# Seven products of blocks instead of eight in the MLP's second product, over three quarters of its weight rows

## The reference

```python
h = rmsnorm_2(x, g_norm2[l]) * (1.0 + sc2) + sh2
x = x + gt2 * (jnp.square(jax.nn.relu(h @ w1[l])) @ w2[l])
```

## Time and profile before

| | |
|---|---|
| median of 3 runs | 994.14 us (993.88 to 995.94) |
| the profiled execution: its own time | 994.67 us |
| its span, first to last instruction | 992.8 us |
| PE busy | 974.2 us (98%) |
| DVE busy | 656.1 us (66%) |
| ACT busy | 483.6 us (49%) |
| granted TensorE clock, mean | 0.999 |

### The profile page before, as it was taken

The page is one execution under the profiler, slowest core; times in us unless marked ns, Lnnn a source line. Parts: engine busy times, 40 slices in busy tenths (PEclk is TensorE's granted clock), DMA queues, the critical chain, the costliest instruction groups (busy, mean ns, idle before and its releaser), DMA issues.

```text
span 992.8 us, 13022 instructions
## 1 busy us (share of the span) xinstructions
PE 974.2 (98%) x4784; PEld 813.3 (82%) x4784; DVE 656.1 (66%) x1203; ACT 483.6 (49%) x963; POOL 69.9 (7%) x158
## 2 busy tenths in 40 slices
PE   9999999999999999999899999999999999999998
PEld 7878999888888888777788878788888888888886
DVE  6487888869788758367678886875455544445453
ACT  6458777753223445589787554343224214322420
POOL 4001001012112011000000001100000000000000
PEclk9999999999999999999999999999999999999999
DMA  8205131248778415342442226147222232322221
GB/s 299 77 23 183 65 104 58 86 181 329 281 289 318 175 79 154 101 145 80 138 148 65 70 101 254 43 168 151 85 85 85 90 121 85 127 85 85 85 75 53
DMA packets 34080, 129.81 MB, mean 131 GB/s; under 512 B 8905, under 2 KB 8905, under 8 KB 24418
## 3 DMA queue, kind: packets, MB, share of 16 engines
q1 hardware_dynamic: 23538, 98.27, 29.3%
q0 software_dynamic: 7408, 26.75, 7.9%
q10 hardware_dynamic: 3072, 3.98, 1.2%
HBM read 119.45 MB, written 5.27 MB: 126 GB/s over the span
## 4 chain that ended last, share of the span: by engine, by line
PE 82%; DVE 9%; ACT 4%; issue 2%; DMA 2%; POOL 0%; SPq 0%; DVEq 0%; ACTq 0%; POOLq 0%
PE psum L1849 24%; PE psum L1851 24%; PE psum L1850 24%; PE psum L2016 2%; PE psum L1995 2%; PE psum L2045 1%; PE psum L2048 1%; DVE wl L1088 1%; DVE two L1627 1%; PE psum L1883 1%; DVE hl L1128 1%; DMA value_rows<-rows 1%; ACT wh L589 1%; DVE two L1492 1%; DMA raw<-in_wall 1%
## 5 line engine op out<-in xcount | busy, mean ns | idle before, releaser
L1849 PE MATMUL psum<-hh,wh 128*128 128x512 f32 (+1 forms) x720 | 274.0, 381 | 0.7 <-DVE hl L1128 0.6
L1851 PE MATMUL psum<-hh,wl 128*128 128x512 f32 (+1 forms) x720 | 267.4, 371 | 0.0
L1850 PE MATMUL psum<-hl,wh 128*128 128x512 f32 (+1 forms) x720 | 267.2, 371 | 0.0
L589 ACT ACTIVATE wh<-raw 128x512 fp32r<-128x512 f32 x292 | 169.3, 620 | 137.3 <-PE psum L1851 121.7
L1088 DVE TENSOR_TENSOR wl<-raw,wh 128x512 fp32r<-128x512 f32 x292 | 192.1, 683 | 16.7 <-ACT wh L589 16.4
L1849 PEld LDWEIGHTS psum<-hh,wh 128*128 128x128 f32 x720 | 135.3, 188 | 24.3 <-DVE hl L1128 1.6
L1851 PEld LDWEIGHTS psum<-hh,wl 128*128 128x128 f32 x720 | 135.2, 188 | 23.8
L1850 PEld LDWEIGHTS psum<-hl,wh 128*128 128x128 f32 x720 | 135.5, 188 | 21.1 <-issue 1.0
L1849 PE MATMUL psum<-wh,ah 128*128 128x512 f32 x320 | 125.6, 392 | 0.0
L1851 PE MATMUL psum<-wh,al 128*128 128x512 f32 x320 | 124.6, 389 | 0.0
L1850 PE MATMUL psum<-wl,ah 128*128 128x512 f32 x320 | 124.6, 389 | 0.0
(11 more groups left out here) (282 smaller groups left out, 1464.9 us busy)
## 6 DMA issues: line engine op xcount, KB each, us to landing
raw<-in_wall SPq DMA_DIRECT2D x75, 1024.0 KB, 5.0
wa<-in_wada POOLq DMA_DIRECT2D x20, 512.0 KB, 6.3
gt<-in_wada POOLq DMA_DIRECT2D x20, 512.0 KB, 6.4
wb<-in_wada POOLq DMA_DIRECT2D x8, 512.0 KB, 7.7
xt<-in_xcols SPq DMA_DIRECT2D x8, 264.0 KB, 7.8
cb<-c_rows SPq DMA_DIRECT2D x8, 264.0 KB, 3.3
x<-in_x SPq DMA_DIRECT2D x4, 512.0 KB, 10.2
x_kept<-x SPq DMA_DIRECT2D x4, 512.0 KB, 2.8
```

The source lines that it names most:

```text
L589: e.activation(home(w)[0][:, 512 * c:512 * c + 512], raw_of(w, c), ACT.Copy).then_inc(a["wh"], 1)
L1849: e.matmul(out_, lh, rh, start=start, stop=False, skip_group_check=True)
L1850: e.matmul(out_, lh, rl, start=False, stop=False, skip_group_check=True)
L1851: return e.matmul(out_, ll, rh, start=False, stop=stop, skip_group_check=True)
```

## The change

In quarters 0, 1 and 2 the second product is done by Strassen's scheme. With A the squares of a quarter (512 tokens by 1024 hidden) and B its 1024x1024 rows of `w2`, A and B are cut into 2x2 blocks (A11 is 256 tokens by 512 hidden, B11 is 512x512, one unit). PE makes seven products, in this order of numbers: 1, 2, 7, 6, 5, 3, 4.

- Each product is 2 token tiles x 4 k tiles x 3 = 24 matmuls of 128x512.
- Products 1, 2, 3 use the units B11, B21, B22 as loaded. Products 7, 6, 5, 4 use sums and differences of units, each made from the one before in the raw buffers by DVE, in two instructions of 128x1024 (`weight_sum`).
- The activations get their sums too (`halves`): one difference of 256 columns for hidden tiles 0 to 3, three dependent ones for tiles 4 to 7, of which a tile of 768 columns is split again (`s_hi`, `s_lo`).
- Products 3 and 4 stay in banks 4 to 7 over the three quarters. Products 1, 2, 7, 6, 5 are added up over the quarters in SBUF: in quarter 0 by an ACT copy (`first_sum`), in quarters 1 and 2 by a DVE add (`gather`), two instructions for each product.
- In quarter 3, whose product is done as before, DVE combines the seven sums into the four blocks (`blocks`, 14 instructions), multiplies by the gate and adds to `x2` (`add_block`, 16 instructions), and does so again for quarter 3's own product (`add_last`). The eight gated steps at the end of quarters 0 to 2 are gone.
- There is a fourth raw buffer, `raw3`, which lies over `mis`; its first load waits for the last of the table sums. Raw buffers are held until the last sum that needs them has been split (`place`, `freed`). The order of loading in `w2` is B11, B22, B12, B21.
- The slots in which the MLP's lower parts stand are moved by one or so, and some semaphores are merged under one name (`n1` and `n3` into `nsq`, `hh1` and `hh2` into `hh`, `hl1` and `hl2` into `hl`, `tp1` and `tp2` into `tp`).

The diff, cut to its core:

```diff
+PRODUCTS = (1, 2, 7, 6, 5, 3, 4)
+P_BANK = {1: (2, 3), 2: (0, 1), 7: (2, 3), 6: (0, 1), 5: (2, 3), 3: (4, 5), 4: (6, 7)}
+GATHERED = (1, 2, 7, 6, 5)
...
+        for w_ in range(W_MLP + 1, NW):
+            lowers[w_] = {1: (0,), 3: (1,), 5: (2,), 6: (3,)}
...
+                    if place[n] == 3 and nth[n] == 1:
+                        e.wait_ge(v["tile"], 48)
...
+            def hidden_upper(n, part=0):
+                q, m = divmod(n, 8)
+                if q < 3 and (m < 4 or part):
+                    e.wait_ge(v["s"], 16 * q + (m + 1 if m < 4 else 3 * m - 5))
...
+                if part:
+                    e.activation(s_hi[m - 4], s_f[m - 4], ACT.Copy).then_inc(a["sh"], 1)
+                else:
+                    e.activation(ah[:, m, :], hidden_at(n), ACT.Copy).then_inc(a["sh"], 1)
...
+                for r, p in enumerate(PRODUCTS):
+                    w = W_MLP + 11 * q + 4 + r
+                    if q == 0 and r and PRODUCTS[r - 1] in sums:
+                        for b in range(2):
+                            first_sum(PRODUCTS[r - 1], b)
+                    for c in range(4):
+                        upper(w + 1, c)
...
+            def halves(n):
+
+                q, m = divmod(n, 8)
+                f = s_f[m % 4]
+                e.wait_ge(v["r2"], n + 1)
+                if m < 4:
+                    e.tensor_tensor(f[:, 256:512], f[:, 0:256], f[:, 512:768], ALU.subtract).then_inc(v["s"], 1)
+                    return
+                y, c = tmp[:, m % 2, :], 16 * q + 3 * m - 8
+                e.tensor_tensor(f[:, 512:768], f[:, 512:768], y[:, 256:512], ALU.add).then_inc(v["s"], 1)
+                e.wait_ge(v["s"], c + 1)
+                e.tensor_tensor(f[:, 0:256], f[:, 512:768], f[:, 0:256], ALU.subtract).then_inc(v["s"], 1)
+                e.wait_ge(v["s"], c + 2)
+                e.tensor_tensor(f[:, 256:512], y[:, 0:256], f[:, 0:256], ALU.subtract).then_inc(v["s"], 1)
...
+            def weight_sum(q, p):
...
+                for i in range(2):
+                    part = slice(1024 * i, 1024 * i + 1024)
...
+                    e.tensor_tensor(raw_at(dst)[:, part], raw_at(x_)[:, part], raw_at(y_)[:, part], op).then_inc(v["wt"], 1)
+
+            def gather(q, p, b):
+                e.wait_ge(t["w2"], 14 * q + 2 * PRODUCTS.index(p) + b + 1)
...
+                e.tensor_tensor(sums[p][b], sums[p][b], bank[P_BANK[p][b]], ALU.add).then_inc(v["x3"], 1)
...
             for q in range(4):
                 for j in range(4):
...
+                    w = W_MLP + 11 * q + j
+                    if w > W_MLP:
+                        for s_ in range(4):
+                            slot(w, s_)
+                    hidden(8 * q + 2 * j)
+                    if w > W_MLP:
+                        for s_ in range(4, 8):
+                            slot(w, s_)
+                    hidden(8 * q + 2 * j + 1)
...
+                for r, p in enumerate(PRODUCTS):
+                    w = W_MLP + 11 * q + 4 + r
+                    if q and r and PRODUCTS[r - 1] in sums:
+                        for b in range(2):
+                            gather(q, PRODUCTS[r - 1], b)
+                    for c in range(4):
+                        lower(w + 1, c)
+                    if r == 0:
+                        weight_sum(q, 7)
+                    if r in (0, 2, 3):
+                        weight_sum(q, {0: 6, 2: 5, 3: 4}[r])
...
+            def product(q, r):
+                p, w = PRODUCTS[r], W_MLP + 11 * q + 4 + r
+                upper, lower = home(w)
+                for b in range(2):
+                    if p < 3:
+
+                        e.wait_ge(v["r2"], 8 * q + (6 if p == 1 else 8))
+                    elif p > 4:
+                        gathered(q, {7: 1, 6: 2, 5: 7}[p], b)
+                    for k in range(4):
+                        if b == 0:
+                            e.wait_ge(v["wl"], 4 * w + k + 1)
+                            e.wait_ge(v["sl"], n_sl(q, k if p in (1, 7) else 4 + k, p in (5, 6, 3)))
+                        o = slice(512 * k, 512 * k + 512)
+                        ins = three(bank[P_BANK[p][b]], *factor(p, k, b), upper[:, o], lower[:, o],
+                                    k == 0 and (p in sums or q == 0), k == 3 and (p in sums or q == 2))
+                    ins.then_inc(t["w2"], 1)
```

More of the change, by code:

```diff
@@ L117, in program @@
     gates = nc.dram_tensor("gate_rows", (2, D), F32, kind="Internal").ap()
-    NW = len(units)
+    NW = 44 + 3 * 11 + 8
     W_V, W_ZA, W_1, W_G = 0, 2, 4, 12
@@ L131, in program @@
         over += [("w1", 8 * q_ + 2 * j + 2) for j in range(4)]
-        over += [("half", 6 + 2 * q_), ("w2", 8 * q_ + 4), ("half", 7 + 2 * q_), ("w2", 8 * q_ + 8)]
+        over += ([("w2", 14 * q_ + 2 * r + 2) for r in range(7)] if q_ < 3 else
+                 [("half", 6), ("w2", 46), ("half", 7), ("w2", 50)])
     assert len(over) == NW
@@ new lines, in hidden, with first_sum @@
+            def hidden(n):
+                relu_sq(n)
+                if n == 5:
+                    e.wait_ge(v["mod"], 3)
+                    for c in (0, 4):
+                        e.dma_start(gates[1, 128 * c:128 * c + 512].rearrange("(c p) -> p c", p=128),
+                                    mod[:, 40 + c:44 + c], allow_slow_non_contiguous=True).then_inc(d["g1"], 16)
+                hidden_upper(n)
+                if n < 24 and n % 8 > 3:
+                    hidden_upper(n, 1)
+            def first_sum(p, b):
+                e.wait_ge(t["w2"], 2 * PRODUCTS.index(p) + b + 1)
+                e.activation(sums[p][b], bank[P_BANK[p][b]], ACT.Copy).then_inc(a["acc"], 1)
@@ L1064, in _ @@
[L1064 to L1077, removed]
-                            e.wait_ge(v["x3"], 2 * (24 + 4 * ch + i) + 2)
-                            e.dma_start(out[128 * i:128 * i + 128, 512 * ch:512 * ch + 512],
-                                        x2[:, i, 512 * ch:512 * ch + 512]).then_inc(d["out"], 16)
+                    w = W_MLP + 11 * q + j
@@ L1081, in _ @@
+            for m in range(4):
+                for s_ in range(8):
+                    slot(W_MLP + 37 + m, s_)
+                    if m % 2 and s_ % 2:
+                        ch, i = m // 2, s_ // 2
+                        e.wait_ge(v["x3"], N_X3[3, "+", ch, i])
+                        e.dma_start(out[128 * i:128 * i + 128, 512 * ch:512 * ch + 512],
+                                    x2[:, i, 512 * ch:512 * ch + 512]).then_inc(d["out"], 16)
             e.wait_ge(d["out"], 16 * 8)
@@ new lines, in hidden_lower, with hidden @@
+            def hidden_lower(n, part=0):
+                q, m = divmod(n, 8)
+                e.wait_ge(a["sh"], n_sl(q, m, part) if q < 3 else 36 + m + 1)
+                if part:
+                    dst, src, upper_ = s_lo[m - 4], s_f[m - 4], s_hi[m - 4]
+                else:
+                    dst, src, upper_ = al[:, m, :], hidden_at(n), ah[:, m, :]
+                e.tensor_tensor(dst, src, upper_.bitcast(F32), ALU.subtract).then_inc(v["sl"], 1)
+            def hidden(n):
+                square(n)
+                if n < 24:
+                    halves(n)
+                hidden_lower(n)
+                if n < 24 and n % 8 > 3:
+                    hidden_lower(n, 1)
@@ new lines, in _ @@
+                    if w > W_MLP:
+                        for s_ in range(4):
+                            slot(w, s_)
+                    hidden(8 * q + 2 * j)
+                    if w > W_MLP:
+                        for s_ in range(4, 8):
+                            slot(w, s_)
+                    hidden(8 * q + 2 * j + 1)
+                    if q == 3 and j < 2:
+                        for name in (("u2", "u3", "c12a", "c22"), ("c11", "c12", "c21"))[j]:
+                            for b in range(2):
+                                blocks(name, b)
+                    elif q == 3 and j == 2:
+                        for i in range(4):
+                            add_block(0, i)
@@ L1720, in _ @@
+            for m in range(4):
+                for s_ in range(8):
+                    slot(W_MLP + 37 + m, s_)
+                    if m % 2 and s_ % 2:
+                        add_last(m // 2, s_ // 2)
+                    if m == 0 and s_ % 2:
+                        add_block(1, s_ // 2)
         @block.gpsimd
```

291 lines of the change are left out of this document (189 added, 102 removed).

## The result

The changed kernel takes 998.38 us in the median of 10 runs (996.4 to 1000.24), the kernel before 994.12 us in 10 (993.14 to 995.94). The ratio is 1.004, with a 95% interval of 1.0028 to 1.0051. The forecast was 988.0 in a range of 983.0 to 993.5. The profiled execution is the fastest of the ten, 996.4 us with a span of 994.6.

A forecast was written before the change was run, and what follows sets the result against it. PE alone was taken to set the MLP's pace. 16.3 saved less waits of 4.3, 2.8 and 2.8 gave 6.4 us off the profiled 994.67, so 988.3, or 988.0 for the median; range 983 to 993.5.

The forecast's parts named there:

- Loads: Weight loads into raw buffers: 4.8 us to landing fits, even for the block wanted for product 2 after 684; cost nothing.
- rival D: Clock falls to 1.2 GHz at the turns before product 7: 5.4 us each, 16.3 in three quarters, 1004.3; chance 0.07.
- PE's gain: MLP second product, three quarters: seven block products instead of eight remove 72 matmuls of 0.2267 us, 16.3 us.
- Quarters 1 and 2: Turn from W1 to W2: PE waits 0.1 us before product 2 and 2.7 before product 7, 2.8 lost per quarter.
- Tiles 4 to 7: Hidden tiles of a quarter: DVE's chain takes 5.1 us per tile against PE's 5.44, so it fits with 0.3 to spare.
- The prices of 128x256 and 128x768: DVE instruction times: 0.414 us for 128x256, and 0.96 for 128x768, taken as the middle of 0.69 and 1.23.
- Quarter 0's chain on DVE: From hidden tile 2 to product 7, with eight table sums queued, DVE is never early; PE's waits sum to 4.3 us.
- Quarter 3 and the tail: Quarter 3's combining, 21 us, lies in its five units and costs nothing; the tail after the last matmul stays.
- DVE's total: DVE work in a steady quarter: 68 us in some 84, so the mean is no limit.
- Rivals A and B: A: DVE is ahead, no PE waits, 978, chance 0.10; B: DVE paces the products, 996.5 at 10% more, chance 0.17.
- the 0.9 for faster or no change: Chances for the whole kernel's time: faster (below 992.1) 0.76, within one part in five hundred, 2 us, 0.14.

The follow-up runs named there:

- e1: The changed kernel with ACT's two gate writes moved from hidden tile 5 to hidden tile 9, in quarter 1: 990.81 us, ratio 0.9957.
- e2: The changed kernel with the gate written to memory twice at hidden tile 5, the second time to an unread row: 1002.36 us, one run.
- e4: e1 with the last eight table sums over 128 of their 1024 columns, leaving out seven eighths of them: 988.12 us, ratio 0.9932.
- e6: The changed kernel with the gate write at its old place but in pieces of four neighbouring floats: 990.67 us, one run.
- e3: e1 with DVE's weight sum for product 6 moved behind the lowers of product 7: 984.12 us, ratio 0.9896.
- e8: The changed kernel with only the sum for product 6 moved behind product 7's lowers, gate write at its old place: 995.2 us, ratio 1.0009.

## Why the prediction was wrong

**The step that failed is "Loads".** It said that B21 is wanted after 684 and "4.8 us fits", at the median landing time of the earlier trace rows. The price of that one load was 19.7 us. I had priced all loads by the median and had not asked what stands beside this one. The trace of before would have told. Its 31 loads from 606 us on, and its gate write:

```profile
DMA to landing us min/median/max: 4.6/4.8/13.8
...
674.15 0.95 ACTq L1069 DMA_DIRECT2D gate_rows<-mod  x2
```

The slowest of them, 13.8 us, is the one that was issued at 675.34, 1.2 us behind the write; the write itself took 9.7. The block that it brought was wanted later, so nothing waited. The change took that cover away: it holds the raw buffers longer, frees the fourth at the last table sum, and that same sum is what lets ACT's gate write start. So the write and the two loads are now issued within 1 us of each other, and the second load is wanted for product 2. The pause is 7.0 us longer than e1's and the low clock behind it costs 2.4, while the wait before product 7 (1.5 with its restart) goes: 7.9 in all, which is 12.3 less 4.4.

The sum had a second term at nothing: the clock, rival D, with 0.07. D priced a dip at a product's 24 matmuls, 5.4 us. The dips measured cost less: 2.4 us (12.5 matmuls) behind the pause of 7.7 us, and 1.4 to 1.6 us behind those of 2.4. In the changed kernel's profiled execution the dip stands in quarter 0 and not at the turns, where D had put it; in e2, e4 and e6 it is at the turns of quarters 1 or 2. The books of the fastest run explain 8.1 us of the miss (996.4 against 988.3); the median misses by 10.4, and the 2.3 that remain go with the lower clocks of the other runs. With the load mended, e1's median still is 2.8 above the forecast, for the same reason. The rule of the Trainium skill, TensorE: Matmul & The Clock Gate, HAM oscillation, that the waits between groups of matmuls send the engine back to half clock each time, holds for the long pause here, and for the pauses of 2.4 us only in some executions. Those of 0.15 to 1.2 us never did it in these profiles.

**What held.** PE's gain, 72 x 0.2267 = 16.3: the books of the profiled execution close with it to 0.1 us. Quarters 1 and 2: 2.8 us forecast, 2.85 measured, in the place named (before product 7) and for the reason named (two sums ahead of its lowers; e3). Tiles 4 to 7: they fit, with DVE waiting 0.29 us for each relu, where a margin of 0.3 was forecast. The prices of 128x256 and 128x768, 0.414 and 0.96, came out at 0.425 and 0.959. Quarter 0's chain on DVE: 4.3 forecast, 4.4 measured once the load is there (e1), and e4 shows its cause. In e1, where the load is on time and the clock stayed up, the profiled execution took 987.9 against 988.3 in the sum. Quarter 3 and the tail cost nothing, as said. DVE's total came out at 63 us a quarter in place of 68, since overlapping instructions were counted in full; no step hung on it.

**Rivals A and B** did not come: the waits are those of the forecast, and none stands before products 6, 5 or 3 in the changed kernel. The late load was not among the rivals at all. Of the 0.9 for faster or no change, some belonged to it, as nearly every buffer's release had been moved.

## What to carry to other kernels

When a change holds buffers longer, take away the median from the price of each load and look up the slowest one in the stretch where it will land, and what is in the DMA queues just ahead of it. A write of single floats is small in bytes and long in time; issue it where no load is due, or in longer pieces. And where an engine fills most of another's shadow, order its queue by due times: two instructions moved past each other brought the median down by 3.2 us with the late load (e8) and by 6.7 without it (e1 to e3).

## What the runs showed of the hardware that was not expected

- Behind 1024 single floats written to memory (4 KB), two 1 MB loads landed in 13.6 and 19.7 us instead of 4.8 and 6.9. With a quarter of the elements they landed in 7.4 (the middle of the two). Writes issued 1 us behind the loads cost 2 us or less.
- In the changed kernel the windows show next to no DMA traffic from 693.5 us on, and ACT, which waits for the load, starts only at 697.85. POOL, which waits for the gate write, starts at 698.81, so the two end close together. What they wait for in those 4 us was not found.
- A POOL instruction with two float32 inputs in SBUF (128x1024, 2.46 us) stops DVE instructions whose inputs both lie in SBUF until it ends; one with an input in PSUM ran on at 0.69 us.
- The clock: at 1.00 behind a PE pause of 2.4 us in the changed kernel and e1, at 0.50 for some 3 us behind the same pause in e6, e2 and, in one of its two quarters, e4. Behind the first such pause it fell when PE was at work again, 0.5 us after the restart in e6 and 1.2 us after it in e2; in e4, and behind the second one in e6, it was down when PE restarted.
